# Transposes of queries and keys placed between the last four projections, in a hybrid attention and mixture-of-experts layer

## What is computed

```python
h = rms_norm(x, g_attn)
proj = h @ w_in          # queries, six key/value groups, gates, fox q/k/v, forget logits, merge logits
q_n = rms_norm(q_n.reshape(B, T, 8, 64), qn_nsa)
k_c = rms_norm(compress(kv_n[:, :, 0], ...), kn_cmp)      # 15 blocks of 32 tokens, an MLP of 256
v_c = compress(kv_n[:, :, 1], ...)
k_s, k_w = rms_norm(kv_n[:, :, 2], kn_sel), rms_norm(kv_n[:, :, 4], kn_win)
o_nsa = nsa_mixer(q_n, k_c, v_c, k_s, v_s, k_w, v_w, nsa_gates)   # compressed + selected + window
o_fox = fox_mixer(rms_norm(q_f, qn_fox), rms_norm(k_f, kn_fox), v_f, f_logit, b_forget)
merge = sigmoid(merge_logit + b_merge)
x = x + (merge[0] * (o_nsa @ w_up_nsa) + merge[1] * (o_fox @ w_up_fox)) @ w_out
x = x + moe_ffn(rms_norm(x, g_mlp), ...)   # top 4 of 32 experts, 1024 x 1024 gate, up and down each
```

## Time and profile before

| what | value |
|---|---|
| three runs | 1162.79, 1165.05, 1165.21 us, median 1165.05 |
| the profiled execution | 1163.53 us |
| its span, first to last instruction | 1161.8 us |
| PE busy | 1102.3 us, 95% |
| VectorE, ScalarE, GpSimd busy | 418.5, 174.2, 121.5 us |
| HBM read | 437.30 MB, 377 GB/s over the span |
| mean granted clock of TensorE | 0.990 |

### The profile page before, as it was taken

How to read it: one execution, slowest core, us unless ns; L and a number is a source line. 1 busy time by engine, 2 the same in 40 slices (tenths; PEclk the granted TensorE clock), 3 DMA queues, 4 the chain that set the end, 5 groups by cost and what they waited for, 6 DMA issues and landing times.

```text
span 1161.8 us, 14623 instructions
## 1 busy us (share of the span) xinstructions
PE 1102.3 (95%) x5766; PEld 522.6 (45%) x5766; DVE 418.5 (36%) x938; ACT 174.2 (15%) x364; POOL 121.5 (10%) x108
## 2 busy tenths in 40 slices
PE   8899999999999999999999999999999999999987
PEld 6778888863333333433333333333333333333323
DVE  6763676832313232332222222222222222222223
ACT  5444664320000000000000000000000000000000
POOL 5465446400000000000000000000000000000000
PEclk9998999999989999999999999999999999999999
DMA  7964640989999999999999999999999999999995
GB/s 262 341 210 165 215 146 6 360 346 418 428 427 429 426 428 428 428 429 427 430 428 429 428 429 428 428 429 428 430 426 430 427 430 427 430 428 427 428 427 227
DMA packets 49229, 438.89 MB, mean 378 GB/s; under 512 B 6594, under 2 KB 12806, under 8 KB 24614
## 3 DMA queue, kind: packets, MB, share of 16 engines
q1 hardware_dynamic: 49142, 438.23, 91.1%
q10 hardware_dynamic: 48, 0.13, 0.0%
HBM read 437.30 MB, written 1.05 MB: 377 GB/s over the span
## 4 chain that ended last, share of the span: by engine, by line
PE 56%; DMA 36%; DVE 3%; SPq 3%; issue 1%; ACT 0%; POOL 0%; DVEq 0%; ACTq 0%
PE bank L1699 33%; DMA ring<-in_w_e_up_dram 18%; DMA ring<-in_w_e_gate_dram 15%; PE bank L1679 3%; PE bank L1718 3%; DMA ring<-in_w_e_down_dram 3%; PE bank L1695 2%; PE bank L1493 2%; PE bank L1494 1%; PE bank L1495 1%; SPq L421 1%; DVE w_lo L384 1%; PE bank L1738 1%; DMA ring<-in_w_in_dram 1%; DVE hT_lo L1115 1%; PE bank L1544 1%
## 5 line engine op out<-in xcount | busy, mean ns | idle before, releaser
L1699 PE MATMUL bank<-ring,heads 128*64 128x512 f32 x3008 | 679.2, 599 | 17.9 <-DMA ring<-in_w_e_gate_dram 15.8
L1699 PEld LDWEIGHTS bank<-ring,heads 128*64 128x64 f32 x3008 | 204.5, 137 | 425.9 <-issue 381.7
L1259 DVE TENSOR_SCALAR heads<-bank 128x512 f32<-128x512 f32 x32 | 22.1, 691 | 303.3 <-PE bank L1699 303.3
L1311 DVE TENSOR_TENSOR x<-x,bank 128x512 f32<-128x512 f32 x124 | 79.8, 683 | 140.8 <-PE bank L1718 140.8
L384 POOL TENSOR_TENSOR w_lo<-ring,w_hi 128x512 fp32r<-128x512 f32 (+2 forms) x56 | 99.3, 1790 | 67.6 <-ACT w_hi L647 67.2
L803 ACT ACTIVATE work<-bank 128x256 f32<-128x256 f32 x32 | 12.3, 383 | 500.7 <-PE bank L1731 500.7
L1718 PE MATMUL bank<-heads,work 64*128 64x512 f32 x248 | 73.0, 644 | 0.0
L1679 PE MATMUL bank<-work,xn 128*128 128x128 f32 x512 | 63.8, 279 | 0.0
L647 ACT ACTIVATE w_hi<-ring 128x512 fp32r<-128x512 f32 (+2 forms) x84 | 58.8, 728 | 18.6 <-PE bank L1387 7.1
L1679 PEld LDWEIGHTS bank<-work,xn 128*128 128x128 f32 x512 | 60.9, 195 | 0.8 <-issue 0.8
L1287 DVE COPY heads<-bank 128x512 f32<-128x512 f32 x31 | 21.4, 691 | 83.2 <-PE bank L1738 83.2
(11 more groups left out here) (300 smaller groups left out, 962.3 us busy)
## 6 DMA issues: line engine op xcount, KB each, us to landing
ring<-in_w_e_up_dram SPq DMA_DIRECT2D x64, 2048.0 KB, 32.3
ring<-in_w_e_down_dram SPq DMA_DIRECT2D x64, 2048.0 KB, 30.8
ring<-in_w_e_gate_dram SPq DMA_DIRECT2D x62, 2048.0 KB, 31.1
ring<-in_w_in_dram SPq DMA_DIRECT2D x8, 2048.0 KB, 8.0
spare<-in_w_e_gate_dram SPq DMA_DIRECT2D x2, 2048.0 KB, 15.2
ring<-in_w_out_dram SPq DMA_DIRECT2D x2, 2048.0 KB, 7.9
ring<-in_w_in_dram SPq DMA_DIRECT2D x2, 1024.0 KB, 8.4
ring<-in_w_ck_dram SPq DMA_DIRECT2D x1, 2048.0 KB, 14.7
```

What stands on the lines that cost most here:

```text
L1259: nc.vector.tensor_scalar(e_g, banks[1][:, :], LIMIT, None, ALU.min).then_inc(g_made, 1)
L1311: ins = nc.vector.tensor_tensor(x[:, t, 512 * h:512 * h + 512], x[:, t, 512 * h:512 * h + 512], bank67[:, j % 2, :], ALU.add)
L1699: last = mm(bank[C * half:C * half + C, :], lhs(kk), w[:, k, 512 * half:512 * half + 512], start=(kk == 0 and m == "down"), stop=(kk == KD ...
```

## The change

TensorE's fourteen transposes units are called at other places. Units 0 and 1 stand before projection 8, 2 and 3 behind it, 4 and 5 behind projection 9, 6 and 7 before projection 11, 8 and 9 behind it, 10 and 11 behind the compressed scores, 12 and 13 between merges 1 and 2. The transposes of the compressed probabilities move from behind merge 1 to behind merge 2. ScalarE and VectorE copy the units at the matching places of their lists. ScalarE makes the high part of piece MERGE before its copy of the last projection.

```diff
@@ ScalarE
             for i in range(12):
...
                 act.wait_ge(proj_done, i + 1)
+                if i == 11:
+                    keep_high(MERGE)
...
+                if 7 <= i < 11:
+                    keep_unit_a(2 * (i - 7))
...
-            keep_high(MERGE)
-            for i, u in enumerate((0, 2, 4)):
-                keep_unit_a(u)
-                if i < 2:
-                    keep_high(MERGE + 1 + i)
+            for i in range(2):
+                keep_unit_a(8 + 2 * i)
+                keep_high(MERGE + 1 + i)
             act.wait_ge(cs_max, 1)
             nc.scalar.activation(cp, cp, ACT.Exp).then_inc(cs_exp, 1)
             keep_high(MERGE + 3)
             for c in range(EARLY):
                 keep_merge(c)
-                keep_unit_a(6 + 2 * c)
+                if c == 0:
+                    keep_unit_a(12)
                 if c < EARLY - 1:
                     keep_high(MERGE + 4 + c)
@@ VectorE
             nc.vector.tensor_copy(fk_tok[:, :, :, DH], OB[0][:, 0:16].rearrange("p (t h) -> p t h", t=NT)).then_inc(f_placed, 1)
+            keep_unit(1)
             head_mean(8, HF)
...
             nc.vector.tensor_scalar(ck_r[0:NC, :], ck_ss[0:NC, :], 1.0 / DH, EPS, ALU.mult, ALU.add).then_inc(mean_made, 1)
             n_inv[0] += 1
+            keep_unit(3)
             keep_low_chunks(5, (6, 7))
...
             head_scale(9, 0, HF, fq_tok[:, 1, :, 0:DH])
+            keep_unit(5)
             dve.wait_ge(ck_turned, 1)
...
-            for u in (1, 3, 5):
-                keep_unit(u)
+            keep_unit(7)
+            keep_unit(9)
...
             nc.vector.tensor_tensor(c3, c3, col(csum, NC), ALU.subtract).then_inc(cs_max, 1)
+            keep_unit(11)
             dve.wait_ge(cs_exp, 1)
...
             nc.vector.tensor_tensor(c3, c3, col(csum, NC), ALU.mult).then_inc(cp_made, 1)
-            keep_unit(7)
+            keep_unit(13)
             dve.wait_ge(cp_turned, 1)
             nc.vector.tensor_copy(cpT, S[1][:, 0:T].rearrange("p (t q) -> p t q", t=NT)).then_inc(cpT_made, 1)
-            keep_unit(9)
-            keep_unit(11)
-            keep_unit(13)
@@ TensorE
             mm(OB[0][:, 8:16], upto[:, :], fb[:, 1, :], start=False, stop=True).then_inc(f_summed, 1)
+            pe.wait_ge(proj_read_v, 6)
+            turn_heads(0)
+            turn_heads(1)
             project(8, "fq", 512)
+            turn_heads(2)
+            turn_heads(3)
             pe.wait_ge(hid_made, 1)
...
             project(9, "fq", 512)
+            turn_heads(4)
+            turn_heads(5)
             project(10, "fv", 512)
...
+            pe.wait_ge(proj_read_v, 8)
+            pe.wait_ge(f_placed, 1)
+            turn_heads(6)
+            turn_heads(7)
             project(11, "fv", 512)
...
-            pe.wait_ge(blk_made, 2)
             pe.wait_ge(proj_read_v, 10)
-            pe.wait_ge(f_placed, 1)
-            for n in range(N_WIDE):
-                turn_heads(n)
+            turn_heads(8)
+            turn_heads(9)
...
+            turn_heads(10)
+            turn_heads(11)
             merge(0)
-            turn_heads(6)
-            turn_heads(7)
             merge(1)
+            turn_heads(12)
+            turn_heads(13)
+            merge(2)
             pe.wait_ge(cp_made, 1)
             for t in range(NT):
                 last = nc.tensor.transpose(S[1][:, P * t:P * t + P], cp[:, P * t:P * t + P], ident[:, :])
             last.then_inc(cp_turned, 1)
-            turn_heads(8)
-            turn_heads(9)
-            merge(2)
-            turn_heads(10)
-            turn_heads(11)
             merge(3)
-            turn_heads(12)
-            turn_heads(13)
             pe.wait_ge(cpT_made, 1)
```

More of the change, by code:

```diff
@@ L675, in two, with keep_unit_a @@
                 return ap.unsqueeze(2).to_broadcast([P, G, 2, DH])
+            def keep_unit_a(n):
+                act.wait_ge(turned, n + 1)
+                if n < N_WIDE:
+                    _, dst, gain = WIDE[n]
+                    ins = nc.scalar.activation(dst, TB[0][:, 0:T], ACT.Copy, scale=gain)
+                else:
+                    _, dst, h0, gain = UNITS[n - N_WIDE]
+                    ins = nc.scalar.activation(dst[:, h0:h0 + 2, :], TB[0][0:DE, :].rearrange("p (h t) -> p h t", h=2), ACT.Copy,
+                                               scale=gain[0:DE, :])
+                ins.then_inc(kept_a, 1)
             for i in range(12):
@@ L985, in _, with keep_unit @@
             head_scale(7, 0, HF, fk_tok[:, 1, :, 0:DH])
+            def keep_unit(n):
+                dve.wait_ge(turned, n + 1)
+                if n < N_WIDE:
+                    _, dst, gain = WIDE[n]
+                    ins = nc.vector.tensor_scalar(dst, TB[1][:, 0:T], gain, None, ALU.mult)
+                else:
+                    _, dst, h0, gain = UNITS[n - N_WIDE]
+                    ins = nc.vector.tensor_scalar(dst[:, h0:h0 + 2, :], TB[1][0:DE, :].rearrange("p (h t) -> p h t", h=2),
+                                                  gain[0:DE, :], None, ALU.mult)
+                ins.then_inc(kept_v, 1)
             dve.wait_ge(f_summed, 1)
@@ L1394, in project, with turn_heads @@
                 last.then_inc(proj_done, 1)
+            def turn_heads(n):
+                if n >= 2:
+                    pe.wait_ge((kept_a, kept_v)[n % 2], n // 2)
+                if n < N_WIDE:
+                    for t, src in enumerate(WIDE[n][0]):
+                        last = nc.tensor.transpose(TB[n % 2][:, P * t:P * t + P], src.rearrange("p u d -> p (u d)"), ident[:, :])
+                else:
+                    src, dst, h0, gain = UNITS[n - N_WIDE]
+                    for h in range(2):
+                        for t in range(NT):
+                            last = nc.tensor.transpose(TB[n % 2][0:DE, 256 * h + P * t:256 * h + P * t + P],
+                                                       src[:, t, h0 + h, :], ident[:, :])
+                last.then_inc(turned, 1)
             project(0, "kv", 512)
@@ L1451, in _ @@
             mm(S[1][:, 0:P], spread[:, :], vc16, start=True, stop=True).then_inc(ck_turned, 1)
+            pe.wait_ge(proj_read_v, 8)
+            pe.wait_ge(f_placed, 1)
+            turn_heads(6)
+            turn_heads(7)
             project(11, "fv", 512)
-            def turn_heads(n):
-                if n >= 2:
-                    pe.wait_ge((kept_a, kept_v)[n % 2], n // 2)
-                if n < N_WIDE:
-                    for t, src in enumerate(WIDE[n][0]):
-                        last = nc.tensor.transpose(TB[n % 2][:, P * t:P * t + P], src.rearrange("p u d -> p (u d)"), ident[:, :])
-                else:
-                    src, dst, h0, gain = UNITS[n - N_WIDE]
-                    for h in range(2):
-                        for t in range(NT):
-                            last = nc.tensor.transpose(TB[n % 2][0:DE, 256 * h + P * t:256 * h + P * t + P],
-                                                       src[:, t, h0 + h, :], ident[:, :])
-                last.then_inc(turned, 1)
-            pe.wait_ge(blk_made, 2)
             pe.wait_ge(proj_read_v, 10)
-            pe.wait_ge(f_placed, 1)
-            for n in range(N_WIDE):
-                turn_heads(n)
+            turn_heads(8)
+            turn_heads(9)
             pe.wait_ge(ck_ready, 1)
```

20 lines of the change are left out of this document (removed).

## The result

The change makes the kernel slower by about 5 us: 1170.88 us, median of 10 runs (1166.93 to 1172.93), against 1165.89 for the kernel before, again 10 runs (1161.88 to 1168.54). The ratio is 1.0044, interval 1.003 to 1.0058. The forecast was 1165.2 with a range up to 1167.9, so the result is outside it.

A forecast was written before the change was run, and what follows sets the result against it. PE and DMA share the bound; PE time before the full weight stream moves the end. From 1164.15 us, -6.4 + 3.3 + 3.3 + 0.8 = +1.0 gives 1165.2; range 1161.1 to 1167.9, eight in ten.

The forecast's parts named there:

- part 1: PE before projection 11 through merge 0: 3.1 us idle and half clock of 2.05 and 1.3 go, together -6.4 us.
- part 2: New PE waits among the projections: 0.8 before the compressed hidden products, 2.5 before projection 10; +3.3 us.
- part 4: Clock over projection 10 after the new idle stretch: between 0 and 1.6 us, middle taken, +0.8.
- part 3: Compressed softmax on VectorE held up by GpSimd's low parts through their exclusive port lock: +3.3 us, ends 0 and 5.7.
- the signs that the prediction named: Expected in the changed profile: waits of 0.8, 2.5 and about 2, scores under 2 us, value products within 2 of 114.6.
- the wait before merge 3: PE at the two transposes of the probabilities, which come near 111.8 after merge 2 ends at 109.8: 2.1 us.
- one more piece of 2.4: Upper end for the softmax delay: one further collision with a GpSimd low part, 5.7 us in place of 3.3.
- a wait of 1.2: Merge 2 starts 1.2 us late, since the tanh of merge 0, whose bank it needs, comes near 106.8.
- one of 2.1: PE waits 2.1 us for the probabilities at the two transposes before merge 3.
- the wait of 2.5: PE before projection 10, for VectorE's copy of unit 3: 2.5 us, ends 0 and 5.5.
- Rival R3: Longer half clock over projection 10 or at both projection waits: 3.4 us for 0.8, or +3.6 to +3.8; 1167.9, chance 0.16.

The follow-up runs named there:

- Experiment 2: Changed kernel with each GpSimd low part of merge pieces 0 to 5 made in four quarter-size instructions; 1164.49 us, ratio 0.9988 to the kernel before.
- experiment 4: Changed kernel with only units 0 to 5 moved among the projections, old order behind projection 11; 1169.25 us, ratio 1.0045 to the kernel before.
- experiment 8: Changed kernel with old order behind projection 11, and ScalarE's high parts 4 and 5 held until after the probabilities; 1167.52 us, ratio 1.0018 to the kernel before.
- Experiment 9: Changed kernel with the clamp of the softmax sums done on ScalarE as sum + 1e-30; 1167.00 us, ratio 1.001 to the kernel before.
- experiment 7: Changed kernel with 31 unread products on PE ahead of the wait for the probabilities; 1167.70 us, ratio 1.0015 to the kernel before.
- experiment 3: Changed kernel with VectorE's copy of unit 3 moved right behind low chunk 3; 1166.12 us, ratio 1.0001 to the kernel before.
- Experiment 10: Kernel before with 13 and 6 unread products in PE's idle ahead of units 2 and 4; 1166.82 us, ratio 1.0022 to the kernel before.
- experiment 6: Changed kernel with the two transposes of the probabilities behind merge 3 instead of before it; 1167.09 us, ratio 1.0011 to the kernel before.
- experiment 1: Changed kernel with ScalarE's high parts 4 and 5 made only after the probabilities; 1162.60 us, ratio 0.9978 to the kernel before.
- experiment 5: Changed kernel with high parts 4 and 5 after the probabilities and unit 3's copy behind low chunk 3; 1157.31 us, ratio 0.994 to the kernel before.

## Why the prediction was wrong

By its own steps, on PE's way to the products with the compressed values:

| step | forecast, us | trace of after, us |
|---|---|---|
| part 1, idle removed | -3.1 | -3.1 |
| part 1, half clock removed | -3.3 | -3.1 (scores 3.0 to 1.9, merge 0 4.95 to 2.9) |
| part 2, waits among the projections | +3.3 (0.8 and 2.5) | +3.3 (0.84 and 2.42) |
| part 4, clock over projection 10 | +0.8 | +1.7 (89.89 - 82.64 = 7.25, before 5.54) |
| part 3, softmax late | +3.3 (1.2 and 2.1) | +3.9 (0 and 3.89) |
| half clock over the transposes and merge 3 | nothing | +2.5 (5.61 in place of 3.15) |
| sum | +1.0 | +5.2, of 5.5 found |

The remaining 0.3 was not traced. Of the signs that the prediction named, those up to the scores came as it said; the wait before merge 3 was 3.89 in place of 2, and the four products with the compressed values came 5.5 us after 114.6, where it had allowed 2.

**Parts 1 and 2 were right** in kind and size, and so was the lock of part 3: steps that read two operands of SBUF last about as long as the GpSimd piece that they meet (2.00 and 2.52 us for pieces of 2.4), not a few tenths longer than alone. Experiment 2 confirms it.

**Part 3 counted one collision too few.** It said "VectorE operations that read two operands from SBUF do not run beside it" and so let the clamp pass, which reads one. The clamp took 2.37 us. It had passed in the rows before, but only 0.01 us ahead of GpSimd's piece, and the prediction did not ask what the copy of unit 11 ahead of it would do to that margin. Experiments 4 and 8, without a copy there, show the clamp at 0.17 and 0.18; that the copy makes the difference is read from the traces, no run moved it alone. The missed collision is the end "one more piece of 2.4" which the prediction had named at 5.7: the probabilities came at 114.4, not at 111.8. Of these 2.6 us PE felt 0.6, because it was itself some 1.8 us later at this point than forecast, so that the tanh of merge 0 cost it nothing (merge 2 starts at 107.47, straight behind the transposes). That 3.3 and 3.9 lie so close is therefore in part luck: the forecast had a wait of 1.2 that did not come, and one of 2.1 that was 3.89. Experiment 9 shows the clamp by itself: off VectorE, it gives back 2.1 us of the probabilities and 2.7 of the wait. The section of the Trainium skill that the prediction leaned on ("SBUF — State Buffer", "Who interferes with whom") says that a tensor_scalar can enter a mode that takes both ports, and can then contend as well, while a tensor_reduce never does on this chip. Both agree with the trace here, 2.37 us for the clamp and 0.42 for the reduction that ran beside a piece at 103.15; the prediction used the rule for two operands only.

**The step that was missing is the clock behind that wait.** The prediction had a term for the clock behind the wait of 2.5 alone; the wait before the transposes it priced by its length. A wait of 3.89 took 3.89 + 2.5 here, and experiment 7, which keeps PE busy while the probabilities come as late, gives those 2.5 back. The three kernels with a wait of 3.8 to 3.9 us before these transposes and nothing to fill it (after, experiments 3 and 10) show half clock behind it; experiment 4, with 3.31, and experiments 6 and 9, with waits of up to 1.2, do not. The length of the wait alone does not decide it, as the clock stayed full behind 3.31 us and fell behind 1.78 at another place (experiments 4 and 8). The term of part 4 itself was also low, 0.8 for 1.7. Rival R3 was a half clock, with 3.4 to 3.6 us as its price, but placed over projection 10 or at the waits among the projections. Its mechanism came true at two places: 1.7 us over projection 10, where it was looked for, and 2.5 behind the probabilities, where it was not.

**The range** failed because these two were taken as one case at a time. R3 alone gave 1167.9, one more piece alone 1165.2 + 2.4 = 1167.6. But they come together: the wait that one more piece made 3.89 us long is the one behind which the clock fell. Together they reach 1170, close to the 1170.88 measured.

**The gain of part 1 could not be booked by itself.** Experiment 10 fills the idle and keeps the clock full at the scores and merge 0, and the kernel gets slower. No step of the prediction asked this: what the faster scores and merge 0 would trigger on ScalarE was followed for the change, but not seen as a price of the -3.3. There, 1.1 us won at the tanh of merge 0 sufficed to bring a GpSimd piece into VectorE's chain. With the collisions held off, the gain is to be had: 0.9978 in experiment 1, 0.994 in experiment 5.

**Left open.** The profiled executions differ by 7.3 us, 5.5 of them at 120 us; the medians by 5.0. Of the 1.8 us that come later, 1.6 lie in the last group of products (56 of L1828, L1819 before). It takes 7.91 us in the trace of after, where the granted clock is 0.57 from 1154 to 1158, and 6.26 in the kernel before, at 1.00. It was at half in the traces of experiments 2, 3, 4, 7, 9 and 10 too, and not in those of 1, 5, 6 and 8. Between 120 us and this group the kernels before and after take the same, 1034.2 and 1034.4 us, and so do experiments 1 and 5 (1034.4 and 1034.3): what is lost by the products with the compressed values arrives whole at the end. Experiments 2, 7 and 9 take 1036.2 to 1036.4; in them the clock was at half for some 4 us at 187 to 195 as well. So it was in experiments 6, 8 and 10, and not in the other six traces, all of which have the same wait of 2.02 us there. Nor was it settled why the clock falls behind the wait of 2.42 in some executions (after, experiments 2, 7, 8 and 9) and not in others (1, 4 and 6). Each of these shorter stretches costs 1.6 to 2 us. Whether a kernel's order changes how often they come was not measured, so differences of 2 us between kernels can't be given to one step.

## What to carry to other kernels

Where a chain of short VectorE steps runs beside long GpSimd instructions, count its steps, not its microseconds: each step can cost one whole GpSimd instruction, so either hold the long instructions back until the chain is through (one wait, 0.66% here) or cut them in pieces. Look how closely a step gets in ahead of the other engine before; a small copy put in front of it can lose that. Ask of every wait that is moved or made longer whether the clock will fall behind it, and cost both together. And before a microsecond on the bounding engine is booked as a gain, look for what its lateness had kept apart.

## What the runs showed of the hardware

- A VectorE tensor_scalar with one operand in SBUF, 16 values per row, took 0.17 to 0.18 us where it began 0.01 to 0.02 us ahead of a GpSimd subtraction of 128x1024 (before, experiments 4, 8 and 10), and 2.34 to 2.37 us where it began 0.07 us behind it (after, experiments 1, 3, 5, 6 and 7). A reciprocal of the same 16 values took 0.25 and a reduction 0.42 in both cases.
- Between GpSimd instructions that follow each other without a gap, one VectorE step is let in, and the next waits for the next one: 2.37, 2.00 and 2.52 us for three steps that take 0.17, 0.17 and 0.42 alone. GpSimd pays too, but little: three pieces took 7.26 us among these steps and 7.00 in the kernel before.
- The clock fell to half during or behind a wait of PE of 3.8 to 3.9 us in all three kernels that had one unfilled, and 31 unread products in that wait kept it full. Behind a wait of 3.31 us it stayed full in the one trace that had one, and it fell behind 1.78 (two of two), 2.02 (six of twelve) and 2.42 (five of eight).
- A kernel became slower (1.0022) by filling 2.2 us of idle on its bounding engine with work that nothing waits for.
